# The router of a two-layer MoE step: ranking by comparing all pairs, with the second gate read later

## The reference, cut to what matters

```python
def hier_moe(h, wg, bg, we, be, w1, w3, w2):
    x = h.reshape(-1, D)
    pg = softmax(x @ wg + bg)                       # 4 groups
    pg_top, g_idx = lax.top_k(pg, 1)
    le = (x @ we + be).reshape(-1, 4, 4)            # 4 experts in each group
    le_g = einsum('ng,nge->ne', one_hot(g_idx[:, 0], 4), le)
    pe = softmax(le_g)
    pe_top, e_idx = lax.top_k(pe, 2)
    wts = pg_top * pe_top / sum(pe_top)
    ids = g_idx * 4 + e_idx
    comb = einsum('nk,nke->ne', wts, one_hot(ids, 16))
    a = silu(x @ w1) * (x @ w3) * comb              # per expert
    return a @ w2
```

## Time and profile before

| | |
|---|---|
| median of 3 runs | 786.59 us (786.29 to 787.45) |
| profiled execution, span of its instructions | 785.1 us |
| TensorE busy | 764.6 us, 97% |
| VectorE busy | 343.4 us, 44% |
| ScalarE busy | 177.8 us, 23% |
| HBM traffic | 277.12 MB, mean 353 GB/s |

### The profile page before, as it was taken

How to read it: one execution, slowest core, us unless ns; L and a number is a source line. 1 busy time by engine, 2 the same in 40 slices (tenths; PEclk the granted TensorE clock), 3 DMA queues, 4 the chain that set the end, 5 groups by cost and what they waited for, 6 DMA issues and landing times.

```text
span 785.1 us, 10152 instructions
## 1 busy us (share of the span) xinstructions
PE 764.6 (97%) x3991; PEld 377.2 (48%) x3991; DVE 343.4 (44%) x783; ACT 177.8 (23%) x440; POOL 2.2 (0%) x9
## 2 busy tenths in 40 slices
PE   7999999999999999999999999999999999999997
PEld 3364535545553444444345657645544444345334
DVE  2216188214841742643345412326732643445326
ACT  4111566205521111101112601105221101111111
POOL 0000000000000000000000000000000000000000
PEclk9999999999999999999999999999999999999999
DMA  8979999942899999999999982024599999999994
GB/s 347 427 220 429 430 426 426 427 169 100 330 368 407 425 429 429 427 425 428 425 415 425 425 351 107 1 108 192 203 387 422 427 424 428 428 426 426 425 415 189
DMA packets 32851, 277.12 MB, mean 353 GB/s; under 512 B 7789, under 2 KB 8833, under 8 KB 12833
## 3 DMA queue, kind: packets, MB, share of 16 engines
q1 hardware_dynamic: 32305, 275.02, 85.0%
q10 hardware_dynamic: 432, 1.28, 0.4%
q0 software_dynamic: 64, 0.13, 0.0%
HBM read 274.72 MB, written 1.70 MB: 352 GB/s over the span
## 4 chain that ended last, share of the span: by engine, by line
PE 85%; DMA 5%; DVE 4%; ACT 2%; issue 1%; SPq 1%; DVEq 1%; ACTq 0%
PE bank L2052 27%; PE bank L2077 13%; PE bank L1922 11%; PE bank L2031 5%; PE bank L2083 5%; PE bank L2484 5%; PE bank L2347 4%; PE bank L1861 4%; DMA ring<-in_moe_w 3%; DMA ring<-in_ada_w 3%; PE bank L2308 2%; PE bank L2399 1%; PE bank L2063 1%; PE bank L2420 1%; PE bank L2058 1%
## 5 line engine op out<-in xcount | busy, mean ns | idle before, releaser
L2052 PE MATMUL bank<-ring,Z 128*64 128x512 f32 x1024 | 226.5, 594 | 0.6 <-DMA ring<-in_moe_w 0.6
L2052 PEld LDWEIGHTS bank<-ring,Z 128*64 128x64 f32 x1024 | 72.2, 137 | 137.8 <-issue 135.7
L2077 PE MATMUL bank<-ring,Z 128*64 128x512 f32 (+1 forms) x544 | 114.0, 571 | 0.0
L1922 PE MATMUL bank<-ring,T 128*128 128x512 f32 x192 | 83.1, 592 | 0.0
L2077 PEld LDWEIGHTS bank<-ring,Z 128*64 128x64 f32 x544 | 37.5, 137 | 68.4 <-issue 66.5
L1534 DVE TENSOR_TENSOR Z<-Z,bank 128x512 f32<-128x512 f32 x16 | 11.0, 687 | 120.0 <-PE bank L2052 120.0
L1922 PEld LDWEIGHTS bank<-ring,T 128*128 128x128 f32 x192 | 36.2, 190 | 44.0 <-issue 44.0
L2083 PE MATMUL bank<-ys,Cs 128*128 128x512 f32 (+1 forms) x204 | 52.3, 391 | 1.1 <-DVE ys L1551 1.1
L1564 DVE TENSOR_TENSOR x<-x,bank 128x512 f32<-128x512 f32 x84 | 52.1, 680 | 0.3
L1176 ACT ACTIVATE ys<-wg 128x512 fp32r<-128x512 f32 (+1 forms) x34 | 20.6, 606 | 131.2 <-DVE wg L1546 131.2
L1528 DVE COPY Z<-bank 128x512 f32<-128x512 f32 x24 | 16.6, 692 | 73.8 <-PE bank L2031 73.8
(11 more groups left out here) (249 smaller groups left out, 752.5 us busy)
## 6 DMA issues: line engine op xcount, KB each, us to landing
ring<-in_moe_w SPq DMA_DIRECT2D x62, 2048.0 KB, 15.8
ring<-in_moe_w SPq DMA_DIRECT2D x60, 1024.0 KB, 11.8
ring<-in_ada_w SPq DMA_DIRECT2D x23, 2048.0 KB, 17.9
ring<-in_moe_w SPq DMA_DIRECT2D x16, 512.0 KB, 20.3
ring<-in_a_w_out SPq DMA_DIRECT2D x2, 2048.0 KB, 16.7
ring<-in_f_w_in SPq DMA_DIRECT2D x2, 2048.0 KB, 27.8
ring<-in_f_w_out SPq DMA_DIRECT2D x2, 2048.0 KB, 30.9
ring<-in_ada_w SPq DMA_DIRECT2D x2, 1024.0 KB, 8.2
```

Source lines behind the costliest of these rows:

```text
L1922: last = pe.matmul(b[:, :], T[:, k, i * P:(i + 1) * P], w[:, k, :], start=(k == 0), stop=(k == KT - 1))
L2052: last = pe.matmul(out[BLK * u:BLK * (u + 1), :], xT[:, b, k, s0 + BLK * u:s0 + BLK * (u + 1)], w[:, k, :], start=(k == 0), stop=(k == KT ...
L2077: last = pe.matmul(out, aT[:, k, BLK * u:BLK * (u + 1)], down_columns(w2, k, a, e), start=(k == 0), stop=(k == FC - 1), skip_group_check=True)
```

## The change

- **Logits.** In place of three transposes and a reduction on VectorE, three matmuls with a constant `quarters` (128 x 20, a one where partition modulo 32 is the column) transpose and add the four strips at once. VectorE only copies the 60 columns.
- **Ranking.** The 20 logits of a token are five sets of four: the groups, and the experts of each group. For every pair in a set a difference is taken and compared with 0 or with the smallest normal number (`beats`), which breaks ties; the sum of a row is the place of that logit in its set (0 is the best). `og` is 8 for the best group; `ge` = og - place is 8 for the best expert of the best group and 7 for the second. `Ms` is ge > 6.5, and `M12` is ge equal to 8 and to 7.
- **Later.** The maxima are taken after `Ms`. The differences `dg` and `de` come after the one-hots, and with them the exponentials on ScalarE, which now stand behind the gate reads of LAST_GATE. `gate_parts(LAST_GATE+1)` comes after the one-hots too, ahead of the last `low_part`. On TensorE the reads of LAST_GATE+1 move behind both steps of `first_gather`; both `busy(3)` ahead of `rank` go, `ada_product(20)` stands between the two reads of LAST_GATE, and in layer 1 the second `busy(3)` stays.
- **Constants.** `ones` (128 columns) becomes a memset, `quarters` is new (20 columns), `desc` becomes `beats` (16 columns each).

```diff
@@ TensorE, route
                 for t in range(NT):
-                    last = pe.transpose(b[:, t * P:(t + 1) * P], lrow[:, t * P:(t + 1) * P], ident)
+                    last = pe.matmul(b[:, t * (NG + NE):(t + 1) * (NG + NE)], lrow[:, t * P:(t + 1) * P], con("quarters"),
+                                     start=True, stop=True)
                 last.then_inc(full, 1)
                 tokens_half(l, NT - 1, 1)
                 n = LAST_GATE[l]
                 ada_product(n + 1)
-                done_by(("ada", n))
-                gate_read(n, 0)
-
-                busy(3)
                 b = begin(("rank", l))
...
                 last.then_inc(full, 1)
-                gate_read(n, 1)
-                ada_read(n + 1)
+                done_by(("ada", n))
+                gate_read(n, 0)
                 if l == 0:
                     ada_product(20)
-                else:
+                gate_read(n, 1)
+                if l == 1:
                     busy(3)
@@ TensorE, first_gather, after the second step
                     last.then_inc(s["gathered"], 1)
+                    ada_read(LAST_GATE[l] + 1)
@@ ScalarE
                 high_part(l, 2)
                 n = LAST_GATE[l]
-                act.wait_ge(g_shifted, 2 * l + 2)
+                ada_product(n + 1)
+                ada_read(n)
+                act.wait_ge(g_shifted, l + 1)
                 act.activation(eg, dg, ACT.Exp)
                 act.activation(ee, de, ACT.Exp).then_inc(g_exp, 1)
-                ada_product(n + 1)
-                ada_read(n)
                 ada_read(n + 1)
                 if l == 0:
                     ada_product(20)
                 moe(l)
@@ VectorE, route
-                emptied_inc(dve.tensor_reduce(lg, parts, AX.X, ALU.add))
+                emptied_inc(dve.tensor_copy(lg.rearrange("p t n -> p (t n)"), b[:, 0:NSET * EPG]))
+                settle()
+                sets = lg.rearrange("p t (s e) -> p (t s) e", e=EPG)
+                dve.tensor_tensor(ahead, bc(sets.unsqueeze(2), NSET, EPG, EPG), bc(sets.unsqueeze(3), NSET, EPG, EPG),
+                                  ALU.subtract)
+                settle()
+                beats = con("beats").rearrange("p (e f) -> p e f", e=EPG).unsqueeze(1)
+                dve.tensor_tensor(ahead, ahead, bc(beats, NSET, EPG, EPG), ALU.is_ge)
+                settle()
+                add_reduce(place, ahead)
                 settle()
...
+                dve.tensor_scalar(og, place[:, :, 0:NG], 0.0, 8.0, ALU.is_equal, ALU.mult)
+                settle()
+                dve.tensor_tensor(ge.rearrange("p t (g e) -> p t g e", g=NG), every(og),
+                                  place[:, :, NG:].rearrange("p t (g e) -> p t g e", g=NG), ALU.subtract)
+                settle()
+                dve.tensor_scalar(Ms[:, 0:NT, :], ge, 6.5, None, ALU.is_gt).then_inc(ms_ready, 1)
+                for c in range(2):
+                    dve.tensor_scalar(M12[:, c], ge, 8.0 - c, None, ALU.is_equal)
                 dve.tensor_reduce(mg, lgg, AX.X, ALU.max)
                 dve.tensor_reduce(ml, le, AX.X, ALU.max)
                 settle()
-                dve.tensor_tensor(dg, lgg, bc(mg.unsqueeze(2), NT, NG), ALU.subtract).then_inc(g_shifted, 1)
...
-                dve.tensor_tensor(Ms[:, 0:NT, :], M12[:, 0], M12[:, 1], ALU.add).then_inc(ms_ready, 1)
-                gate_parts(LAST_GATE[l] + 1)
...
                 slots_of_tokens()
                 one_hot(pairs[l], QUAD)
+                dve.tensor_tensor(dg, lgg, bc(mg.unsqueeze(2), NT, NG), ALU.subtract)
+                dve.tensor_tensor(de, le, every(ml), ALU.subtract).then_inc(g_shifted, 1)
+                gate_parts(LAST_GATE[l] + 1)
                 low_part(l, NT - 1)
                 if l == 0:
                     gate_parts(20)
@@ VectorE, start
-            dve.tensor_copy(ones_bf, con("ones"))
+            dve.memset(ones_bf, 1.0)
```

More of the change, by code:

```diff
@@ L87, in constant_columns @@
     out["before"] = (p[:, None] < p[None, :]).astype(float)
-    out["ones"] = np.ones((P, P))
     for n in range(2):
@@ L93, in constant_columns @@
     out["row_low"], out["row_sign"] = low, 1 - 2 * low
+    out["quarters"] = (p[:, None] % 32 == np.arange(NG + NE)[None, :]).astype(float)
     rows = {
         "iota": np.arange(QUAD),
-        "desc": np.tile(np.arange(EPG, 0, -1), NG),
+        "beats": np.where(np.arange(EPG)[None, :] < np.arange(EPG)[:, None], 0.0, np.finfo(np.float32).tiny).ravel(),
         "limit": BLK * np.arange(1, NTHR + 1),
@@ L304, in route @@
         t.fill(("tokens", l, 2, 1), "dve", bank=last_tile[1])
-        t.add(("ada", n + 1), "dve", bank=others[1])
+        t.fill(("ada", n + 1), "dve", bank=others[1])
+        t.add(("rank", l), "dve", bank=first)
         t.add(("gate", n, 0), "act", bank=others[0])
-        t.add(("rank", l), "dve", bank=first)
-        t.add(("gate", n, 1), "act", bank=others[0])
-        t.add(("gate", n + 1, 0), "act", bank=first)
-        t.add(("gate", n + 1, 1), "act", bank=others[1])
         if l == 0:
             t.fill(("ada", 20), "dve", bank=7)
+        t.add(("gate", n, 1), "act", bank=others[0])
+        t.empty(("ada", n + 1))
         of_gather[l] = [t.of[t.last[bank]][2:4] for bank in (2, 3)]
@@ L317, in route @@
             t.empty(("ada", 20))
+        t.add(("gate", n + 1, 0), "act", bank=first)
+        t.add(("gate", n + 1, 1), "act", bank=others[1])
     t.add("rows", "dve", bank=0)
@@ L652, in build @@
         mg, sg, pg, p1 = (rtile(NT) for _ in range(4))
-        dg, eg, og, sc4 = (rtile(NT, NG) for _ in range(4))
+        dg, eg, og = (rtile(NT, NG) for _ in range(3))
         ml, se = (rtile(NT, NG) for _ in range(2))
+        place = rtile(NT, NG + NE)
         de, ee = (rtile(NT, NG, EPG) for _ in range(2))
@@ L667, in build @@
         cmp_j = tri_p[:, 0:NOV, :]
-        scratch16 = tri_p.rearrange("p a b -> p (a b)")[:, 0:4 * NT * NE]
-        sc16, o1, o2, le2 = (scratch16[:, NT * NE * i:NT * NE * (i + 1)].rearrange("p (t g e) -> p t g e", t=NT, g=NG)
-                             for i in range(4))
+        NSET = NT * (NG + 1)
+        ahead = tri_p.rearrange("p a b -> p (a b)")[:, 0:NSET * EPG * EPG].rearrange("p (s e f) -> p s e f", s=NSET, e=EPG)
         assert rat[0] <= NH * P
@@ L1436, in route @@
                 settle()
-                dve.tensor_tensor(dg, lgg, bc(mg.unsqueeze(2), NT, NG), ALU.subtract).then_inc(g_shifted, 1)
-                dve.tensor_tensor(de, le, every(ml), ALU.subtract).then_inc(g_shifted, 1)
-                settle()
-                dve.scalar_tensor_tensor(sc4, dg, 0.0, bc(descending, NT, NG), ALU.is_equal, ALU.mult)
-                dve.scalar_tensor_tensor(flat(sc16), flat(de), 0.0, by_expert, ALU.is_equal, ALU.mult)
-                settle()
-                dve.tensor_reduce(sg, sc4, AX.X, ALU.max)
-                dve.tensor_reduce(ml, sc16, AX.X, ALU.max)
-                settle()
-                dve.tensor_tensor(og, sc4, bc(sg.unsqueeze(2), NT, NG), ALU.is_equal)
-                dve.tensor_tensor(o1, sc16, every(ml), ALU.is_equal)
-                settle()
-                dve.scalar_tensor_tensor(flat(le2), flat(o1), LOWEST, lg[:, :, NG:], ALU.mult, ALU.add)
-                dve.tensor_tensor(o2, con("desc").rearrange("p (g e) -> p g e", g=NG).unsqueeze(1).to_broadcast([P, NT, NG, EPG]),
-                                  every(og), ALU.mult)
-                settle()
-                dve.tensor_reduce(ml, le2, AX.X, ALU.max)
-                settle()
-                dve.tensor_tensor(sc16, le2, every(ml), ALU.is_equal)
-                settle()
-                dve.tensor_tensor(sc16, sc16, o2, ALU.mult)
-                settle()
-                dve.tensor_reduce(pg, flat(sc16), AX.X, ALU.max)
-                dve.tensor_tensor(M12[:, 0].rearrange("p t (g e) -> p t g e", g=NG), o1, every(og), ALU.mult)
-                settle()
-                dve.tensor_tensor(M12[:, 1], flat(sc16), bc(pg.unsqueeze(2), NT, NE), ALU.is_equal)
-                settle()
-                dve.tensor_tensor(Ms[:, 0:NT, :], M12[:, 0], M12[:, 1], ALU.add).then_inc(ms_ready, 1)
-                gate_parts(LAST_GATE[l] + 1)
                 b = stage_bank(("rank", l), dve)
```

4 lines of the change are left out of this document (removed).

## The result

The changed kernel takes **789.65 us** (788.36 to 790.68, 4 runs) where the kernel before, run beside it, takes 786.59 (median of three executions; a fourth took 2768.89 us and is left out of the ratio; with it the median is 787.02): ratio **1.0038, 95% interval 1.0025 to 1.0050**, about 3 us slower. Predicted were 789.4 us, 787.2 to 792.2, and slower with 0.75. The profiled execution is the fastest of the four, 788.36 us with a span of 786.4; its granted clock is 1.00 in the route stage and the experts of both layers by the table by stretch further down and its like.

A forecast was written before the change was run, and what follows sets the result against it. TensorE, busy 97% of the 785.1 us span, was taken as the bound. Layer 0 +1.9, layer 1 +1.0 and constants -0.1 make +2.8, span 787.9; with 1.5 carried over, 789.4 us, range 787.2 to 792.2.

The forecast's parts named there:

- The shorter ranking: VectorE's route stage: the chain up to Ms takes 2.19 us instead of 4.22, a gain of 2.03.
- The router: TensorE's three matmuls in place of transposes: logits 0.1 us later, bounds 0.1 earlier to 0.3 later.
- What comes back: VectorE ahead of the last low_part: shifts and gate part cost 0.87 us, leaving low_part 1.13 us earlier per layer.
- The moved gate reads: Behind the gather: xT and gate_parts(20) wait for the copies; experts start 1.9 us later in layer 0, 1.0 in layer 1.
- (b): Rival, no stall ahead of the experts: the gate copies are hidden, 2.4 us gained, 784.2 us; chance 0.07.
- (d): Rival, VectorE's ranking is not shorter because broadcast operands run slower: 1.1 us a layer more, 791.6 us; chance 0.05.
- (c): Rival, gain and loss nearly cancel: layer 0 at +1.1, layer 1 at +0.4, 788.0 us or less; chance 0.14.
- The exponentials: ScalarE, with their table load behind the gate copy: cost nothing; at most 1.7 us if that cover were gone.
- VectorE's later plan: VectorE's work up to weighted starts 2.6 us later; 2.6 us of idle cover remain before the experts, nothing paid.
- The constants: Kernel start: 108 fewer columns to load, 0 to 0.13 us gained, taken as 0.1.
- The wait for weights at 410.65: TensorE's 0.56 us wait among the layer 0 experts: stays and gives nothing back, as the weights' stream shifts by 1.9 us.
- (a): Rival, TensorE's clock falls after the new idle time: 1.7 to 2.4 us lost once or twice, 791.1 to 794; chance 0.12.

The follow-up runs named there:

- e3: The changed kernel with only ScalarE's scaling of the gate 20 row moved ahead of the exponentials: 788.17 us, ratio 1.0021.
- e4: The changed kernel with TensorE's second gate read moved into the first gather, ahead of its wait for the last low_part: 784.29 us, ratio 0.9973.
- e8: The changed kernel with the LAST_GATE+1 reads and parts back in their old places, exponentials still behind the first two gate copies: 784.10 us, ratio 0.9968.
- e2: The changed kernel with the LAST_GATE+1 reads and parts back in their old places and the exponentials ahead of those gate copies: 786.97 us, ratio 1.0005.
- e1: The kernel before with only the constants of the changed one: 786.18 us, ratio 0.9994.
- e7: The changed kernel with five (layer 0) and three (layer 1) fill-in matmuls on TensorE behind the gate reads: 788.65 us, ratio 1.0028.
- e11: The changed kernel with the old ranking, the second gate read inside the first gather and the gate 20 row ahead of the exponentials: 787.88 us, ratio 1.0013.
- a0: The changed kernel run again without any edit, beside the kernel before: 791.33 us, ratio 1.0057.

## Why the prediction was right, and where it was not

The forecast, its sign and its main mechanism hold. Step by step:

- **The shorter ranking**: 2.29 us for the predicted 2.19. The two 240-element operations take 0.41 us each, for which I took 0.36 from the 256-element row. The formula of the Trainium skill (VectorE: DVE Perf Modes, the section on the TRN2 errata), 0.407 for 240 elements, was the better of the two, and the measurement decides for it. The step on the sizes failed by 0.1.
- **The router**: 0.29 us later at VectorE's read for 0.1, at the upper bound of 0.3, since each of the six records takes 0.14 us. L1458, which answers to the old L1471, is 3.80 us behind the router's start instead of 5.59: 1.79 us earlier for 2.0. The two terms make 0.29, of which 0.08 came back between `Ms` and L1458 (0.63 us for the predicted 0.71).
- **What comes back**: dg, de and the gate part cost 0.86 (206.11 to 206.97) for 0.87. `low_part` 0.92 and 0.95 us earlier for 1.13.
- **The moved gate reads**: +2.02 for +1.9 in layer 0, +1.13 for +1.0 in layer 1; both are the predicted numbers plus the 0.2 lost above, less a little. The two waiters are as forecast: the last addition of gate 20 in layer 0 (e3 takes it away), xT in layer 1. Rival (b) is refuted, and (d) too, since the ranking is as short as forecast; (c) needed +1.1 and +0.4; e4 and e8 show from the other side that the place of these reads is the whole loss.
- **The exponentials** are free, as predicted, within the bound of 1.7 us without their cover: in e2 layer 0 takes 12.31 where e8 takes 11.64, 0.67 us, which is nearly all of the 0.71 that the ranking gains there.
- **VectorE's later plan**: 2.49 us of idle time are left ahead of L1395 at 222.72; predicted 2.6.
- **The constants**: the start gained nothing that shows, but the experts' gather matmuls came closer together, by 0.42 us over the first six pairs in each layer of e1, an effect that no step of mine held. By the traces that is 0.84 us; e1's time, 0.5 us less with an interval from 1.2 less to 0.2 more, neither proves nor denies it. 2.02 + 1.13 - 0.84 = 2.31 us is then the change without the clock, or 2.07 with the waits for weights (0.32 us for 0.56); e7 measures 2.2 (ratio 1.0028).
- **The wait for weights at 410.65 stays**: wrong. In the changed kernel's layer 0 it is gone, and layer 1 has one of 0.32 us at 735.82. Other traces have such waits at 384.09 (0.44, e8), at 410.80 (0.67, e11) or none at all (e1, with the old router). So the time at which the route stage ends doesn't decide it alone.
- **The clock**: the step that was weighed worst. I had the idle times (2.5 and 1.4 us, measured 2.42 and 1.15) and the price (1.7 to 2.4, measured 1.7) but gave the case 0.12, because an idle time of 1.24 us elsewhere had left the clock alone. That row said nothing of two waits that stand close together. I also took the page's row of nines for full clock in every slice, and named a value under 1 in it as the sign of (a). A nine is 90% or more, and the run with the fall reads nines too, so the sign would have missed it. The fall is there in seven of nine executions by the mean clock, costs about 1.7 us in the one that was traced, and comes and goes between executions of the same program.

So 789.4 was hit in part by luck. By the mean clock the kernel takes 788.4 to 788.9 without the fall and 790.3 to 791.4 with it, and the first four runs were two of each, so that their median fell between the two. The small terms (the 0.84 us beside the constants, for which I had 0.1) made the one lower than my sum, the clock the other higher.

## What to carry to other kernels

Put a step that only hands over data into a wait that the engine has anyway, not behind the last work ahead of a stage: here the same two matmuls cost next to nothing in one place and over 5 us in the other, mostly through the copies that another engine then does ahead of what the stage waits for. When an engine's chain gets shorter, look at what was in its shadow: in layer 0 the shorter ranking gains nothing until the exponentials are moved, too. And count a new idle time on TensorE together with its neighbours: in two traces here two close ones were followed by 3 us at half clock after the work had come back, in others they were not. Look for that in a table by short stretches and in the mean clock of every execution, not in one trace's page.

## What the hardware showed that I had not expected

- The granted clock fell to 0.50 for about 3 us in a0, beginning between 214.0 and 214.5, about 1 us after TensorE was busy again (213.30), after idle times of 1.16 and 2.42 us with 1.9 us of work between them. In the first trace of the changed kernel the same two idle times (1.15 and 2.42) were followed by no fall. After 1.17 and 1.59 us, in layer 1 with 0.75 us some 5 us ahead of them, it did not fall in the traces of the changed kernel, of its second run and of e3, and after 2.47 us not in e2's. After 1.89 and 0.75 us in e11 it did.
- A matmul of 20 fp32 columns took two records of 0.14 us each (0.84 for six), where a transpose of 128 columns took 0.18 (0.55 for three). Cutting the columns to a sixth saved a fifth of a record's time, and there are twice as many records.
- With the constants' columns changed, and so the places in SBUF of other tensors, six pairs of experts took 0.25% less (173.55 for 173.97 us), by gather matmuls that stand closer together (24 in 2.93 us for 3.03). The cause is open; it wasn't tried further.
